# Memory units between the stick-breaking heads, and sums over 2048 instead of 2560 columns a head

## What is computed

```python
def second_block(x, mem, ...):
    x = x + 0.5 * swiglu_2(rmsnorm(x, ffn1_norm), ffn1_w_gu, ffn1_w_down)
    proj = rmsnorm(x, mix_norm) @ w_in
    hg_q, hg_f, hg_i, hg_g, sb_q, sb_k, sb_v = split(proj)
    o_hg = hgrn2_mixer(hg_q, hg_f, hg_i, hg_g, lb, hg_gnorm)      # 4 heads of 128, recurrent, in chunks
    o_sb = stick_breaking_mixer(sb_q, sb_k, sb_v, sb_gnorm)       # 8 heads of 64
    x = x + concatenate([o_hg, o_sb]) @ w_out
    x = x + memory_cross_attention(rmsnorm(x, mem_q_norm), rmsnorm(mem, mem_kv_norm), w_q, w_kv, w_o)
    x = x + 0.5 * swiglu_2(rmsnorm(x, ffn2_norm), ffn2_w_gu, ffn2_w_down)
    return rmsnorm(x, final_norm)

def stick_breaking_mixer(q, k, v, gnorm):       # per head; before = (s < t)
    z = q @ k.T * scale
    log_one_minus = where(before, log_sigmoid(-z), 0)
    between = cumsum(log_one_minus, reverse=True) - log_one_minus     # the sum over s < j < t
    weights = exp(where(before, log_sigmoid(z) + between, -inf))
    return head_rmsnorm(weights @ v)

def memory_cross_attention(h, m, w_q, w_kv, w_o):      # m: 256 rows of memory, 4 heads of 256
    q = h @ w_q
    k, v = split(m @ w_kv)
    return (softmax(q @ k.T / 16) @ v) @ w_o
```

## Time and profile before

| | us |
|---|---|
| median of three runs | 2531.74 |
| lowest and highest of them | 2530.05, 2534.24 |
| the profiled execution, its own time | 2530.41 |
| its span, first to last instruction | 2528.6 |
| TensorE busy | 2443.9 (97%) |
| VectorE busy | 1246.6 (49%) |
| ScalarE busy | 896.1 (35%) |
| GpSimd busy | 70.6 (3%) |
| chain that ended last, TensorE's share | 87% |

### The profile page before, as it was taken

How to read it: one execution, slowest core, us unless ns; L and a number is a source line. 1 busy time by engine, 2 the same in 40 slices (tenths; PEclk the granted TensorE clock), 3 DMA queues, 4 the chain that set the end, 5 groups by cost and what they waited for, 6 DMA issues and landing times.

```text
span 2528.6 us, 30307 instructions
## 1 busy us (share of the span) xinstructions
PE 2443.9 (97%) x12278; PEld 2034.2 (80%) x12278; DVE 1246.6 (49%) x1493; ACT 896.1 (35%) x1207; POOL 70.6 (3%) x80
## 2 busy tenths in 40 slices
PE   7989999999999999999999999999888999999998
PEld 6657888888899788888788888799866987888886
DVE  6687533357736543332444431546585645444423
ACT  3353333313344343331333321344444444333311
POOL 0210000000012000000000000000000000000000
PEclk9999999998999999999999999999988999999999
DMA  8125522363323122222222222221100322222221
GB/s 347 59 86 215 194 104 100 150 258 125 104 96 97 67 83 100 100 100 100 79 94 93 100 100 100 94 86 67 68 17 17 119 98 73 93 100 91 91 101 66
DMA packets 40408, 267.36 MB, mean 106 GB/s; under 512 B 4379, under 2 KB 5659, under 8 KB 9219
## 3 DMA queue, kind: packets, MB, share of 16 engines
q1 hardware_dynamic: 31248, 219.87, 24.2%
q0 software_dynamic: 5696, 40.37, 4.2%
q10 hardware_dynamic: 3378, 5.91, 0.8%
HBM read 263.90 MB, written 2.24 MB: 105 GB/s over the span
## 4 chain that ended last, share of the span: by engine, by line
PE 87%; DVE 7%; ACT 4%; issue 1%; DMA 0%; DVEq 0%; SPq 0%; ACTq 0%
PE bank L225 25%; PE bank L226 25%; PE bank L227 25%; DVE w_lo L212 1%; ACT w_hi L208 1%; PE bank L2107 1%; PE bank L328 1%; PE bank L2190 1%; PE bank L2202 1%; PE bank L1827 1%; DVE work L452 1%; PE bank L256 1%; DVE work L436 1%; PE bank L257 1%; PE bank L262 1%
## 5 line engine op out<-in xcount | busy, mean ns | idle before, releaser
L225 PE MATMUL bank<-h_hi,w_hi 128*128 128x512 f32 x1832 | 724.2, 395 | 5.4 <-DVE w_lo L212 2.2
L226 PE MATMUL bank<-h_lo,w_hi 128*128 128x512 f32 x1832 | 716.4, 391 | 0.0
L227 PE MATMUL bank<-h_hi,w_lo 128*128 128x512 f32 x1832 | 716.4, 391 | 0.0
L212 DVE TENSOR_TENSOR w_lo<-raw,w_hi 128x2048 fp32r<-128x2048 f32 x192 | 440.0, 2291 | 501.9 <-ACT w_hi L208 501.9
L208 ACT ACTIVATE w_hi<-raw 128x2048 fp32r<-128x2048 f32 x192 | 366.3, 1908 | 430.8 <-PE bank L227 425.6
L225 PEld LDWEIGHTS bank<-h_hi,w_hi 128*128 128x128 f32 x1832 | 346.0, 189 | 84.0 <-issue 6.7
L227 PEld LDWEIGHTS bank<-h_hi,w_lo 128*128 128x128 f32 x1832 | 345.8, 189 | 73.1
L226 PEld LDWEIGHTS bank<-h_lo,w_hi 128*128 128x128 f32 x1832 | 346.0, 189 | 71.8 <-issue 1.4
L227 PE MATMUL bank<-g_hi,w_lo 128*128 (+1 forms) x704 | 273.9, 389 | 0.0
L225 PE MATMUL bank<-g_hi,w_hi 128*128 (+1 forms) x704 | 273.9, 389 | 0.0
L226 PE MATMUL bank<-g_lo,w_hi 128*128 (+1 forms) x704 | 273.9, 389 | 0.0
(11 more groups left out here) (298 smaller groups left out, 2760.7 us busy)
## 6 DMA issues: line engine op xcount, KB each, us to landing
raw<-stream SPq DMA_DIRECT2D x192, 1024.0 KB, 4.8
work<-stream POOLq DMA_DIRECT2D x19, 1024.0 KB, 7.0
h_plain<-stream POOLq DMA_DIRECT2D x16, 1024.0 KB, 5.4
work<-stream SPq DMA_DIRECT2D x13, 1024.0 KB, 12.3
work<-mlstm_rows ACTq DMA_DIRECT2D x8, 512.0 KB, 5.0
x<-xT SPq DMA_DIRECT2D x1, 2048.0 KB, 9.6
outT<-work SPq DMA_DIRECT2D x8, 256.0 KB, 2.2
work<-mlstm_rows ACTq DMA_DIRECT2D x8, 192.0 KB
```

The lines of the kernel that those rows point to most:

```text
L212: nc.vector.tensor_tensor(w_lo[:, slot(m), :], raw[:, slot(m), :], w_hi[:, slot(m), :], ALU.subtract).then_inc(lo_split, 1)
L225: nc.tensor.matmul(out, stationary[0], moving[0], start=first, stop=False)
L226: nc.tensor.matmul(out, stationary[0], moving[1], start=False, stop=False)
L227: return nc.tensor.matmul(out, stationary[1], moving[0], start=False, stop=last)
```

## The change

1. The seven memory units (four of keys, three of values) move in `PLAN` from behind `mix_out` to between `mix_in` and `mix_out`. Each is cut in four pieces that TensorE runs within one step of the stick-breaking heads, u = i - 2. They accumulate in bank 7, and ScalarE evacuates them (`evacuate`) and makes the next unit's high half at the start of the next step; VectorE makes the low half between `e` and `l`.
2. Squares and scaling of the memory move to GpSimd (`Memory.gpsimd`), its root to exp and log (`root_and_high`), its load to the end of `mix_in`; its tiles lie in the place of `h_hi` and `h_lo`.
3. The sums behind the keys go from the last block to the first. For block a they take the triangle on block a, the ones on the diagonal part of block a + 1, and the ones on what GpSimd has added up of the later blocks (`later3`, `later2`): 128 + 384 + 640 + 896 = 2048 columns.
4. `neg_strict` is added by GpSimd. On VectorE the updates of head i - 1 come after `l` of head i.
5. The mixers' norms take exp and log for the root (`LogTail`) and are split into `mixed_hi` and `mixed_lo`; the values go to bank 6 alone. `mix_out` begins its first unit while the last rows are turned.
6. The query norm of the memory attention is applied to the scores (`QueryNorm`): the chunks of `x` times the gain are split directly beside `mix_out`, and no row is spread. The attention begins behind one unit of queries; its 16 steps keep their order.

```diff
-        ("ffn1", FFN_UNITS), ("ffn2", FFN_UNITS), ("mix_in", 14), ("mix_out", 4), ("mem", 12),
+        ("ffn1", FFN_UNITS), ("ffn2", FFN_UNITS), ("mix_in", 14), ("mem_kv", 7), ("mix_out", 4), ("mem", 5),
...
+            def sum_behind(self, pe, h, i):
+                a, n = TB - 1 - i, TB * h + i
+                if i == 0:
+                    pe.wait_ge(self.s_l, h + 1)
+                if i >= 2:
+                    pe.wait_ge(self.s_later, 2 * h + i - 1)
+                if n >= 2:
+                    pe.wait_ge(self.s_x, n - 1)
+                l, out = self.l[h % 2], bank[:, 4 + n % 2, :]
+                last = nc.tensor.matmul(out[:, a * P:S], table("tri"), l[:, self.seg(a)], start=True, stop=(a == TB - 1))
+                if a < TB - 1:
+                    last = nc.tensor.matmul(out[:, (a + 1) * P:(a + 2) * P], ones, l[:, self.diag(a + 1)], start=False,
+                                            stop=(a == TB - 2))
+                if a == 1:
+                    last = nc.tensor.matmul(out[:, 3 * P:S], ones, self.later3, start=False, stop=True)
+                if a == 0:
+                    last = nc.tensor.matmul(out[:, 2 * P:S], ones, self.later2, start=False, stop=True)
+                last.then_inc(self.s_suf, 1)
...
+                for i in range(self.H + 2):
+                    u = i - 2
+                    if i < self.H:
+                        self.score(pe, i)
+                    if i == 0:
+                        hg.sum_values(pe, hg.H - 1)
+                        pe.wait_ge(hg.s_out, hg.H)
+                        mem.sum_squares(pe)
+                        continue
+                    if 0 <= u < 7:
+                        mem.piece(pe, u, 0)
+                    if u >= 0:
+                        self.sum_values(pe, u)
+                    if i == self.H + 1:
+                        break
+                    if 0 <= u < 7 and i < self.H:
+                        mem.piece(pe, u, 1)
+                    for n in range(TB):
+                        self.sum_behind(pe, i - 1, n)
+                        if n == 1 and 0 <= u < 7:
+                            mem.piece(pe, u, 1 if i == self.H else 2)
+                    if i == self.H:
+                        for b in range(4):
+                            hg.tail.turn(pe, b)
+                        mem.piece(pe, u, 2)
+                    if 0 <= u < 7:
+                        mem.piece(pe, u, 3)
...
             def vector(self, dve, st):
...
                         dve.wait_ge(self.s_z, h + 1)
                         if h >= 2:
                             dve.wait_ge(self.s_o, h - 1)
...
                         nc.vector.scalar_tensor_tensor(e, z, -1.0, z, ALU.mult, ALU.max).then_inc(self.s_abs, 1)
...
+                    if 3 <= i < self.H:
+                        split_next_lo(dve, mem.m_kv + i - 3)
                     if h < self.H:
...
                         dve.wait_ge(self.s_ln, h + 1)
                         st.link(nc.vector.scalar_tensor_tensor(l, z, 0.0, e, ALU.max, ALU.add))
...
+                    h = i - 1
+                    if 0 <= h < self.H:
+                        for a in range(TB - 1, -1, -1):
+                            n = TB * h + TB - 1 - a
+                            dve.wait_ge(self.s_suf, n + 1)
+                            z = self.z[h % 2][:, self.seg(a)]
+                            nc.vector.scalar_tensor_tensor(z, bank[:, 4 + n % 2, a * P:S], -1.0, z, ALU.mult,
+                                                           ALU.add).then_inc(self.s_x, 1)
...
+                    if i == 1:
+                        hg.tail.gate_rows(dve, 3)
+                        split_next_lo(dve, mem.m_kv - 1)
+                        mem.low(dve)
...
             def scalar(self, act, st):
...
                 for i in range(self.H + 2):
+                    if 3 <= i <= self.H:
+                        mem.evacuate(act, i - 3)
+                        split_next_hi(act, mem.m_kv + i - 3)
+                    if i == 0:
+                        hg.copy_out(act, hg.H - 1)
+                    h = i - 2
+                    if h >= 0:
+                        act.wait_ge(self.s_nx, h + 1)
+                        nc.scalar.activation(self.z[h % 2], self.z[h % 2], ACT.Exp).then_inc(self.s_a, 1)
                     h = i
                     if h < self.H:
                         e = self.e[h % 2]
                         act.wait_ge(self.s_abs, h + 1)
                         st.link(nc.scalar.activation(e, e, ACT.Exp, scale=-1.0))
                         nc.scalar.activation(e, e, ACT.Ln, bias=1.0).then_inc(self.s_ln, 1)
...
+                    if i == 1:
+                        mem.root_and_high(act, st)
...
+            def add_later(self, pool, h):
+
+                l = self.l[h % 2]
+                pool.wait_ge(self.s_l, h + 1)
+                if h:
+                    pool.wait_ge(self.s_suf, TB * h)
+                nc.gpsimd.tensor_tensor(self.later3, l[:, self.OFF[2] + P:self.OFF[2] + 2 * P], l[:, self.diag(3)],
+                                        ALU.add).then_inc(self.s_later, 1)
+                l1 = l[:, self.OFF[1] + P:self.OFF[1] + 3 * P]
+                nc.gpsimd.tensor_tensor(self.later2[:, 0:P], l1[:, 0:P], l[:, self.diag(2)], ALU.add)
+                pool.wait_ge(self.s_later, 2 * h + 1)
+                nc.gpsimd.tensor_tensor(self.later2[:, P:2 * P], l1[:, P:2 * P], self.later3,
+                                        ALU.add).then_inc(self.s_later, 1)
+
+            def gpsimd(self, pool):
+                self.add_later(pool, 0)
+                for h in range(self.H):
+                    if h + 1 < self.H:
+                        self.add_later(pool, h + 1)
+                    pool.wait_ge(self.s_x, TB * h + TB)
+                    z = self.z[h % 2]
+                    for a in range(TB):
+                        ins = nc.gpsimd.tensor_tensor(z[:, self.diag(a)], z[:, self.diag(a)], table("neg_strict"),
+                                                      ALU.add)
+                    ins.then_inc(self.s_nx, 1)
...
+            def gpsimd(self, pool):
+                pool.wait_ge(mem_loaded, 16)
+                nc.gpsimd.tensor_tensor(self.sq, self.mt, self.mt, ALU.mult).then_inc(self.s_sq, 1)
...
+                nc.gpsimd.tensor_tensor(t, mt, gain.unsqueeze(2).to_broadcast([P, KC, N_MEM]),
+                                        ALU.mult).then_inc(self.s_scaled, 1)
+                pool.wait_ge(self.s_scaled, 1)
+                pool.wait_ge(self.s_root, 1)
+                nc.gpsimd.tensor_tensor(t, t, self.rstd.unsqueeze(1).to_broadcast([P, KC, N_MEM]),
+                                        ALU.mult).then_inc(self.s_scaled, 1)
...
+            def root_and_high(self, act, st):
+                act.wait_ge(self.s_ms, 1)
+                st.link(nc.scalar.activation(self.logs, bank[:, 7, 0:N_MEM], ACT.Ln, bias=eps, scale=1.0 / D))
+                nc.scalar.activation(self.rstd, self.logs, ACT.Exp, scale=-0.5).then_inc(self.s_root, 1)
+                act.wait_ge(self.s_scaled, 2)
+                nc.scalar.activation(mem_hi.rearrange("p a n -> p (a n)"), self.t, ACT.Copy).then_inc(self.s_hi, 1)
...
+            def piece(self, pe, u, j):
+
+                if j == 0:
+                    pe.wait_ge(lo_split, self.m_kv + u + 1)
+                    pe.wait_ge(self.s_lo, 1)
+                    if u:
+                        pe.wait_ge(self.s_kv, u)
...
+            pool.wait_ge(unit_used, FIRST_UNIT["mem_kv"])
+            pool.dma_start(memory.mt, memT[:, :]).then_inc(mem_loaded, 16)
+            memory.gpsimd(pool)
+            mix.sb.gpsimd(pool)
```

More of the change, by code:

```diff
@@ L572, in scalar @@
                 self.take_root(act)
-                act.wait_ge(row_done, self.n + 1)
+                act.wait_ge(row_done, self.rows)
                 nc.scalar.activation(inv_rows[:, :], bank[:, self.ROW, :], ACT.Copy).then_inc(self.rows_done, 1)
@@ L2305, in tensor, with __init__, take_inverse @@
                 self.sb.tensor(pe)
-                self.hg.tail.tensor(pe)
+        class QueryNorm(Norm):
+            deferred, spreads = True, False
+            def __init__(self, scale, before):
+                super().__init__(scale, None, 4, before)
+                self.sq = area(18432, KC, S)
+                self.scores_by = small[:, 488:488 + TB]
+            gain, low = Deferred.gain, Deferred.low
+            def take_inverse(self, dve, st):
+                dve.wait_ge(root_done, self.n + 1)
+                nc.vector.reciprocal(self.inv, self.root).then_inc(inv_done, 1)
+                dve.wait_ge(inv_done, self.n + 1)
+                st.link(nc.vector.tensor_scalar(self.scores_by, self.inv, 256 ** -0.5, None, ALU.mult))
         class Memory:
@@ new lines, in sum_squares @@
+            def sum_squares(self, pe):
+                pe.wait_ge(self.s_sq, 1)
+                for k in range(KC):
```

(11 more changed lines are left out.)

397 lines of the change are left out of this document (187 added, 210 removed).

## The result

The kernel after takes 2561.91 us (median; 2559.81 to 2562.42), beside 2531.59 us for the kernel before on the same chip (four runs each): ratio 1.0118, 95% interval 1.0106 to 1.0130. It is 30.3 us slower. The forecast was 2552, 20.3 us slower, with a range of 2534 to 2566. Direction and mechanism came out as forecast; a third of the loss, 10 us, was missing from the sum.

The account below looks back on a forecast made before the run. TensorE, busy 97%, bounds the kernel, but the loop through the other engines sets the changed steps. 0.4 + 6.8 + 15.5 - 16.4 - 0.9 = +5.4, plus 14.6 of clock, +20.0 us: 2552, range 2534 to 2566.

Parts of the forecast that it names:

- The loop: Steps of heads 3 to 7: chain through the engines takes 19.15 us against 16.04, +15.5 us over five steps.
- The clock: TensorE behind each 4.9 us gap: half clock costs 2 us a step, 12 for six, plus 2.6 at the start.
- The start: Up to the third head's scores: 12 us gap for the memory's preparation replaces 8.12, +0.4 us, plus 2.6 of clock.
- GpSimd's squaring: Memory preparation at the start: squaring 2048 columns on GpSimd takes 4.5 us, up to 6.7 at the slow rate.
- The third head's step: Waits for VectorE's low half of the memory, then the loop: 22.7 us against 15.9, +6.8 us.
- The end: Last step through the first `mix_out` unit: T + 32.3 us, 48.7 before, -16.4 us.
- 1 (no clock lost): TensorE in the steps: gaps cost no clock, time 2537 us (+5.4); chance 0.15.
- 2 (GpSimd late): GpSimd's small additions from 0.65 us up delay `neg_strict`, and scaling may slow the start: 2564 us; chance 0.12.
- 3 (2512, TensorE's own pace): Head steps: loop not closed, TensorE's own work sets 15.2 us a step, no clock lost: 2512 us; chance 0.14.
- 4: Sums behind: the change doesn't act, as the 2048 columns lie beside the loop; part of the forecast, no separate chance.
- third sum, fourth sum, piece 3: TensorE's work behind VectorE's update, closing the step: 1.07, 1.5 and 1.45 us, from T + 14.95 to T + 19.15.

Follow-up runs that it names:

- number 3: Kernel after, with six unread 384-column matmuls on TensorE filling the gap ahead of the third sum of heads 1 to 6: 2549.61 us.
- Number 5: Kernel after, with the second scaling of the memory done by VectorE instead of GpSimd: 2559.69 us.
- Number 10: Kernel after, updates ahead of `l`, GpSimd's mask first, memory scaled on VectorE, 2560 columns without additions, sums first block to last: 2512.12 us.
- number 7: Kernel after, with updates ahead of `l`, GpSimd's mask ahead of its additions, and the memory's second scaling on VectorE: 2534.97 us.
- number 11: Kernel after, updates ahead of `l`, GpSimd's mask first, memory scaled on VectorE, 2048 columns, sums from first block to last: 2514.35 us.
- number 9: Kernel before, with only the order of the sums and updates turned round, last block to first, 2560 columns: 2566.73 us.
- Number 12: Kernel after, with sums and updates taken from the first block to the last, 2048 columns and additions kept: 2551.38 us.
- number 2: Kernel after, with VectorE's updates ahead of `l` and GpSimd's mask ahead of its additions for the next head: 2533.52 us.
- number 8: Kernel after, updates ahead of `l`, GpSimd's mask order turned, memory scaled on VectorE, 2560 columns without GpSimd's additions: 2531.32 us.

## Why the prediction was right, and what it missed

- The loop. Forecast 19.15 us a step at the full clock, and one gap of 4.9 us a head ahead of the third sum, ended by VectorE's update. Measured 19.15 to 19.37 us with the clock kept up (number 3) and gaps of 4.94. The links fit too: in the step that begins at T = 1946.26 VectorE's copies begin at T + 6.33 (forecast 6.3), its masks end at T + 14.60 (14.6), and the third sum begins at T + 14.95 (14.95). That was read link by link from the rows; it was right.
- The clock. Forecast 2 us a step; from 1881.76 to 1987.6 the five steps take 105.9 us, forecast 5 x 21.15 = 105.75, and number 3 puts the clock at 1.9 us in each. That there would be a loss was worked out. The 2 was a choice between 0 and 4, and that it came so close is luck. In every step of the table above the granted clock falls behind the gap and comes back up before the next one, 0.81 to 0.92 in the mean of a step. The Trainium skill, "TensorE: Matmul & The Clock Gate", section "HAM oscillation", says that such a wait puts TensorE back to half rate at every tile. The trace agrees: the third sum, right behind the gap, takes 1.62 us each time and 0.88 in number 3.
- The start was mis-sized: forecast 3.0 us with its clock (0.4 + 2.6), measured 7.1 (1855.15 against 1848.46, and this execution runs 0.45 us early at that point). The step that failed is that VectorE's instructions were taken at the lengths of the earlier trace rows, where nothing ran on GpSimd. Followed in the trace, with those 0.45 us: the root is there 2.0 us late, because the absolute value of head 0 takes 3.86 us instead of 1.49 beside GpSimd's first scaling and all behind it shifts; the second scaling, 4.92 us instead of 4.6, and its hand-over add 0.5; the masks of head 1, 5.86 us instead of 0.90, hold VectorE's update 1.4 us beyond what GpSimd does; and the sums behind take 0.3 more. Together that is the missing 4.1 us, read from one trace. Number 5 tests the masks alone: 4.96 us less for them and, with the scaling now on VectorE, 2.7 us at the third head's scores. The prediction named the Trainium skill's sentence on shared SBUF interfaces ("GPSIMD Engine Reference", "Key points") and gave it no price.
- GpSimd's squaring was taken too long, 4.5 us against 3.59 measured, and `memT` too late, 6.6 against 5.2; neither is on the path, since TensorE comes to the squares only at 1826.90, behind the values of the first mixer. The Trainium skill's 4497 ns ("GPSIMD Engine Reference", section 3.1, an addition of this size) is too high for these multiplications too (3.59 and 3.60 us); the measurement decides.
- The third head's step was mis-sized: forecast 22.7 + 2 = 24.7, measured 26.6. The trace shows where the 1.9 us are:

```profile
1861.85 0.55 PE L227 MATMUL bank<-mem_hi,w_hi 128*128 128x256 f32 x1 [4.25 <-DVE mem_lo L2500]
...
1862.87 1.27 ACT L2346 ACTIVATE work<-work 128x1280 f32<-128x1280 f32 x1 [13.06 <-POOL work L2401]
...
1864.54 2.79 PE L2214 MATMUL bank<-work 128*128 128x64 f32 x20
```

The memory's low half is there 6.7 us after the third head's scores instead of 6.1. The first memory piece behind that wait takes 2.7 us instead of 1.45, at half clock, a wait whose clock the sum had at nothing. `neg_strict` takes 5.79 us instead of 2, but isn't on this path: the weights are ready at 1864.14, before TensorE comes to the values.
- The end was mis-sized: forecast 32.3 us from the last step, measured 35.8 (to the end of the first `mix_out` unit at 2023.4, forecast near 2015). I had it at full clock without a wait behind step 8's; the timeline has

```profile
2005.14 4.29 PE L2214 MATMUL bank<-work 128*128 128x64 f32 x20 [1.78 <-ACT work L2346]
```

a wait of 1.78 us ahead of the last values, and the values at half clock, 4.29 for 2.44 us: 3.6 us together.
- Sum: 4.1 + 1.9 + 3.5 = 9.5 us over the forecast's 20, and spans that differ by 29.4.
- The rivals. 1 (no clock lost) fell with number 3. 2 (GpSimd late) gave the nearer number, 2564, by another way: `neg_strict` takes 1.7 to 2.1 us in the later steps, 0.42 to 0.53 for each of its four additions and not 0.65 or more, but GpSimd's scalings did add at the start. 3 (2512, TensorE's own pace) is wrong for this kernel. Number 10, with VectorE's order and that of the sums turned, the memory's scaling moved and 2560 columns, takes 2512.12; that it meets the rival's number is in part luck, since its steps are 14.90 us and not 15.2. 4 held: 2048 columns give 4.3 us here, hardly more than the noise, 0.8 us a step in number 7 while the clock is up, and nothing in number 11.
- What I didn't see: I followed the loop with "third sum, fourth sum, piece 3" behind the update and took that order as given. In the earlier trace rows the wide sums stand ahead of the wait and 1.14 us behind it; the change reverses that, for the additions' sake, and numbers 9, 10, 11 and 12 put the reversal at 35, 19, 21 and 10.5 us, in four surroundings and with what the clock does included. So these amounts can't be added to the 28.4 us of the two queues. None of the rivals named it.

## What to carry to other kernels

Where two banks are used in turn and a consumer frees them, the order of the producer's pieces has a price of its own. In this kernel it paid, all four times it was tried, to put the large ones ahead of the first wait and the small ones behind it. An edit that needs the other order has to bring more than it costs (here 4.3 us for the columns, 10.5 for the order). And where an interleaving leaves TensorE gaps, write the loop down engine by engine, in each queue's order, before counting saved work: three orders and one moved instruction made 2562 into 2514 us with the same arithmetic (number 11).

## What the runs showed of the hardware

- VectorE and GpSimd hold each other up far more than I expected. Four 128-column masks of VectorE (two inputs in SBUF): 0.90 us alone, 5.86 beside a GpSimd instruction of 4.92 us, and 0.90 again without it (number 5). An operation of 1280 columns: 1.49 and 3.86 us. GpSimd's four small masks: 1.69 to 2.13, and 5.79 us beside two VectorE subtractions of 2.54 us (a subtraction of that size takes 2.28 otherwise). In numbers 2, 7, 8, 10 and 11 the masks of both engines overlap in a step, 3.02 us on GpSimd and 1.82 on VectorE. It looks like waiting for the other's whole instruction rather than sharing; no run isolates that.
- GpSimd on float32, two inputs: 3.59 us for 2048 columns, 0.46 us for 128 (up to 0.90 beside VectorE).
- TensorE's granted clock falls behind each of a series of gaps of 4.9 us (0.84 to 0.92 over a step). Behind gaps of 2 us it falls in some steps: in none of four in number 8 (gaps of 1.98), in one of four in number 2 and in two of four in number 7 (2.08). The length of the gap alone doesn't decide it. Number 12 has 1.00 over a step with a gap of 3.53 us and 0.84 over later ones, and number 9, with gaps of 0.67 and 1.8 to 2.6 us a head and no memory units between, has 0.68 to 0.88.
